# Sample states of a Mamba-2 layer: the sums over old states beside the SSD groups, the new states made in the gate and up blocks from a second read

## What is computed

```
h_new = exp(dt * A) * h_old + dt * B * x     -> output ssm_sample
y     = C . h_new + d_skip * x
```

## Time and profile before

| | |
|---|---|
| median of 3 runs | 2010.57 us (2007.6 to 2012.75) |
| profiled execution, its own time | 2014.25 us |
| its span in the profile | 2012.5 us |
| busy PE, DVE, ACT, POOL | 1912.3, 1208.4, 870.3, 202.3 us |
| mean granted TensorE clock | 0.982 |
| HBM read, written | 388.01 MB, 18.63 MB |

### The profile page before, as it was taken

How to read it: one execution, slowest core, us unless ns; L and a number is a source line. 1 busy time by engine, 2 the same in 40 slices (tenths; PEclk the granted TensorE clock), 3 DMA queues, 4 the chain that set the end, 5 groups by cost and what they waited for, 6 DMA issues and landing times.

```text
span 2012.5 us, 36117 instructions
## 1 busy us (share of the span) xinstructions
PE 1912.3 (95%) x15147; PEld 1801.3 (90%) x15147; DVE 1208.4 (60%) x1620; ACT 870.3 (43%) x1449; POOL 202.3 (10%) x124
## 2 busy tenths in 40 slices
PE   7999999997989999799899999999999999999997
PEld 5999998996888787668699989999999999999997
DVE  4367788799996655563266345655655655533434
ACT  5444455544454443452244445444444444433332
POOL 1144343443000000000000000000000000000000
PEclk9999999998999999899899999999999999999999
DMA  6578876876779697957465535555555555655452
GB/s 205 158 247 298 284 243 214 279 241 215 204 215 289 205 296 210 306 171 235 141 187 171 190 126 184 181 182 189 176 181 189 177 180 189 205 163 180 154 170 96
DMA packets 377331, 408.73 MB, mean 203 GB/s; under 512 B 10480, under 2 KB 346736, under 8 KB 376080
## 3 DMA queue, kind: packets, MB, share of 16 engines
q1 hardware_dynamic: 376608, 405.63, 63.7%
q0 software_dynamic: 208, 0.67, 0.2%
q10 hardware_dynamic: 352, 0.12, 0.0%
HBM read 388.01 MB, written 18.63 MB: 202 GB/s over the span
## 4 chain that ended last, share of the span: by engine, by line
PE 74%; DVE 10%; DMA 6%; SPq 4%; issue 3%; ACT 2%; ACTq 0%; POOL 0%; DVEq 0%; POOLq 0%
PE gemm L1548 23%; PE gemm L1549 22%; PE gemm L1550 22%; DVE w_lo L1091 3%; DMA bc<-bc_row 3%; PE side L1515 2%; DVE st L1085 1%; PE side L1787 1%; DVE conv_out L1085 1%; ACT w_hi L713 1%; SPq L494 1%; SPq L460 1%; DMA out_conv_sample<-crow 1%; DMA out_ssm_sample<-st 1%; PE side L1516 1%
## 5 line engine op out<-in xcount | busy, mean ns | idle before, releaser
L1091 DVE TENSOR_TENSOR w_lo<-raw,w_hi 128x1024 fp32r<-128x1024 f32 (+1 forms) x562 | 733.6, 1313 | 634.4 <-ACT w_hi L713 634.1
L1548 PE MATMUL gemm<-x_hi,w_hi 128*128 128x264 f32 x3344 | 978.1, 292 | 72.5 <-DVE w_lo L1091 71.1
L1549 PE MATMUL gemm<-x_lo,w_hi 128*128 128x264 f32 x3344 | 960.6, 287 | 0.0
L1550 PE MATMUL gemm<-x_hi,w_lo 128*128 128x264 f32 x3344 | 959.1, 287 | 0.0
L713 ACT ACTIVATE w_hi<-raw 128x1024 fp32r<-128x1024 f32 (+1 forms) x562 | 579.5, 1042 | 440.0 <-PE gemm L1550 438.6
L1548 PEld LDWEIGHTS gemm<-x_hi,w_hi 128*128 128x128 f32 x3344 | 641.5, 192 | 99.8 <-DVE w_lo L1091 67.4
L1549 PEld LDWEIGHTS gemm<-x_lo,w_hi 128*128 128x128 f32 x3344 | 642.5, 192 | 0.7 <-issue 0.5
L1550 PEld LDWEIGHTS gemm<-x_hi,w_lo 128*128 128x128 f32 x3344 | 639.5, 191 | 0.0
L1549 PE MATMUL gemm<-g_lo,w_hi 128*128 128x264 f32 x704 | 200.6, 285 | 0.0
L1548 PE MATMUL gemm<-g_hi,w_hi 128*128 128x264 f32 x704 | 200.2, 284 | 0.0
L1550 PE MATMUL gemm<-g_hi,w_lo 128*128 128x264 f32 x704 | 200.0, 284 | 0.0
(11 more groups left out here) (285 smaller groups left out, 1488.9 us busy)
## 6 DMA issues: line engine op xcount, KB each, us to landing
raw<-in_w_in SPq DMA_DIRECT2D x104, 1024.0 KB, 6.1
raw<-in_w_gate SPq DMA_DIRECT2D x44, 1024.0 KB, 5.1
raw<-in_w_up SPq DMA_DIRECT2D x44, 1024.0 KB, 5.1
raw<-in_w_down SPq DMA_DIRECT2D x40, 1024.0 KB, 5.4
kv<-in_cache_k SPq DMA_DIRECT2D x64, 512.0 KB, 5.9
kv<-in_cache_v SPq DMA_DIRECT2D x128, 256.0 KB, 4.3
raw<-in_w_ssm_out SPq DMA_DIRECT2D x16, 1024.0 KB, 7.4
raw<-in_w_out SPq DMA_DIRECT2D x16, 1024.0 KB, 5.4
```

Of the source, the lines that this page charges most:

```text
L1091: v.tensor_tensor(w_lo[:, s, 0:blk.kts, cols], raw[:, s, 0:blk.kts, cols], w_hi[:, b % RING, 0:blk.kts].bitcast(fp32), ALU.subtract).then_ ...
L1548: mm(out, w_hi[:, b % RING, k], pr.hi[:, x], start=(x == 0), stop=False)
L1549: mm(out, w_hi[:, b % RING, k], pr.lo[:, x], start=False, stop=False)
L1550: ins = mm(out, w_lo[:, s, k, cols], pr.hi[:, x], start=False, stop=(x == pr.kt - 1))
```

## The change

- `states` keeps only the sum over the old state: SP loads the state and the two C rows (`crows`, 128 KB) at `max(STATE[m]-6, SSD[2r]+10)`; ACT does nothing; DVE at `STATE[m]+1` waits for the load, makes `stx = st * C` and the sum. No store.
- What is missing in the sum is added per quarter: DVE multiplies the samples' B and C (`bcp`, after the convolution of c), PE sums over the partitions with `ones` at `SSD[2j]`, ACT copies to `bcd` at `+3`, and `sample_u` has three more short steps and the decay `a`.
- `new_states` makes and stores the states in the gate and up blocks, `FS[m] = B_FF + 12 + 5*m`: SP loads the state again into `st2[m % 2]` with the two B rows (`brows`, 128 KB) at `FS-4`; ACT at `FS` scales it by a in place; DVE at `FS+1` adds `B * (dt x)`, four steps; SP stores at `FS+4`.

```diff
-        bc = at("bc", [P, 2, 4, P], fp32, T0 + 8 * K)
+        crows = at("crows", [P, 4, 2, P], fp32, T0 + 8 * K)
...
+        FS = [B_FF + 12 + 5 * m for m in range(4 * NB)]
...
-                    if b == STATE[m] + 3:
-                        sp.wait_ge(st_sum, m + 1)
-                        sp.dma_start(state_rows(ho, n, r), st[:, m % 3]).then_inc(st_out[m % 3], 16)
-                    if b == STATE[m] - 3:
+                    if b == max(STATE[m] - 6, SSD[2 * r] + 10):
...
-                        wait(sp, st_out[m % 3], 16 * (m // 3))
+                        wait(sp, st_sum, m - 2)
                         sp.dma_start(st[:, m % 3], state_rows(hs, n, r)).then_inc(st_in[m % 3], 16)
-                        rows = bc_row[r].rearrange("(w b) n -> b w n", b=NB)[n]
-                        wait(sp, st_sum, m - 1)
-                        sp.dma_start(bc[:, m % 2], rows.partition_broadcast(P)).then_inc(st_in[m % 3], 16)
+                        rows = bc_row[r].rearrange("(w b) n -> b w n", b=NB)[n, 2:4]
+                        sp.dma_start(crows[:, m % 3], rows.partition_broadcast(P)).then_inc(st_in[m % 3], 16)
+
+            def new_states(b):
+
+                for m in range(4 * NB):
+                    r, n = m // NB, m % NB
+                    if b == FS[m] + 4:
+                        sp.wait_ge(s2_sum, m + 1)
+                        sp.dma_start(state_rows(ho, n, r), st2[:, m % 2]).then_inc(s2_out[m % 2], 16)
+                    if b == FS[m] - 4:
...
+                        wait(sp, s2_out[m % 2], 16 * (m // 2))
+                        sp.dma_start(st2[:, m % 2], state_rows(hs, n, r)).then_inc(s2_in[m % 2], 16)
+                        rows = bc_row[r].rearrange("(w b) n -> b w n", b=NB)[n, 0:2]
+                        sp.dma_start(brows[:, m % 2], rows.partition_broadcast(P)).then_inc(s2_in[m % 2], 16)
...
+                        if g % 2 == 0:
+                            func(bcd[:, g // 2], side[2][:, 384:400].rearrange("p (t b) -> p t b", b=NB)).then_inc(bd_cp, 1)
...
-            def states(b):
+            def new_states(b):
...
-                    if b == STATE[m]:
-                        r, n = m // NB, m % NB
-                        act.wait_ge(sx_mul, r + 1)
-                        act.wait_ge(st_in[m % 3], 32 * (m // 3 + 1))
-                        wait(act, st_sum, m)
+                    if b == FS[m]:
+                        r, n, s = m // NB, m % NB, m % 2
+                        act.wait_ge(s2_in[s], 32 * (m // 2 + 1))
                         for t in range(4):
-                            ins = func(stx[:, t, :], bc[:, m % 2, t // 2, :], scale=xdts[:, 4 * r + t, n:n + 1])
-                        ins.then_inc(stx_done, 1)
+                            ins = func(st2[:, s, t, :], st2[:, s, t, :], scale=scal[:, 4 * r + t, NB + n:NB + n + 1])
+                        ins.then_inc(s2_dec, 1)
...
-                        dve.wait_ge(stx_done, m + 1)
-                        for t in range(4):
-                            ins = stt(st[:, s, t, :], st[:, s, t, :], scal[:, 4 * r + t, NB + n:NB + n + 1], stx[:, t, :],
-                                      ALU.mult, ALU.add)
-                        drained(ins)
...
+                        dve.wait_ge(st_in[s], 32 * (m // 3 + 1))
+                        wait(dve, st_sum, m)
...
+                    if b == FS[m] + 1:
+                        r, n, s = m // NB, m % NB, m % 2
+                        dve.wait_ge(s2_dec, m + 1)
+                        for t in range(4):
+                            ins = stt(st2[:, s, t, :], brows[:, s, t // 2, :], xdts[:, 4 * r + t, n:n + 1], st2[:, s, t, :],
+                                      ALU.mult, ALU.add)
+                        ins.then_inc(s2_sum, 1)
```

More of the change, by code:

```diff
@@ L203, in bass_hybrid_decoder_layer @@
         r2b = at("r2b", [P, T], fp32, E0 + 6 * TB)
+        st2 = at("st2", [P, 2, 4, P], fp32, J1 + 2944)
+        brows = at("brows", [P, 2, 2, P], fp32, E0 + 9 * K)
         rdiag = at("rdiag", [P, 3, P], fp32, E0 + 7 * TB)
@@ L332, in bass_hybrid_decoder_layer @@
         st_in = [sem(f"st_in{s}") for s in range(3)]
-        st_out = [sem(f"st_out{s}") for s in range(3)]
+        s2_in = [sem(f"s2_in{s}") for s in range(2)]
+        s2_out = [sem(f"s2_out{s}") for s in range(2)]
         MASKS = 16
@@ L583, in side_work @@
                 states(b)
+                new_states(b)
                 key_loads(b)
@@ L605, in _ @@
                     sp.dma_start(o["y_sample"][:, 0, cols], y1s[:, cols]).then_inc(y_out, 16)
-            for s in range(3):
-                sp.wait_ge(st_out[s], 16 * len(range(s, 4 * NB, 3)))
+            for s in range(2):
+                sp.wait_ge(s2_out[s], 16 * 2 * NB)
             sp.wait_ge(k_out, 48)
@@ L1054, in side_work @@
                 ssd(b)
-                states(b)
+                new_states(b)
                 softmax(b)
@@ L1221, in conv_finish @@
                             .then_inc(xbc_done, 1)
+                    if pr.kind == "c":
+                        j = pr.idx
+                        conv_ready(dve, conv_tile("c", j, 1))
+                        wait(dve, bd_cp, j)
+                        mul(bcp[:, :, :], bct[:, j % 2, 0:2, TP:T], bct[:, j % 2, 2:4, TP:T]).then_inc(bp_done, 1)
                     if pr.kind == "x" and pr.idx % 2:
@@ L1322, in states, with new_states @@
                         r, n, s = m // NB, m % NB, m % 3
-                        dve.wait_ge(stx_done, m + 1)
-                        for t in range(4):
-                            ins = stt(st[:, s, t, :], st[:, s, t, :], scal[:, 4 * r + t, NB + n:NB + n + 1], stx[:, t, :],
-                                      ALU.mult, ALU.add)
-                        drained(ins)
-                        cb = bc[:, m % 2, 2:4, :].unsqueeze(2).to_broadcast([P, 2, 2, P])
+                        dve.wait_ge(st_in[s], 32 * (m // 3 + 1))
+                        wait(dve, st_sum, m)
+                        c = crows[:, s].unsqueeze(2).to_broadcast([P, 2, 2, P])
                         drained(mul(stx[:, :, :].rearrange("p (g t) n -> p g t n", g=2),
-                                    st[:, s].rearrange("p (g t) n -> p g t n", g=2), cb))
+                                    st[:, s].rearrange("p (g t) n -> p g t n", g=2), c))
                         v.tensor_reduce(out=ysam[:, 4 * r:4 * r + 4, n], in_=stx[:, :, :], axis=AX.X, op=ALU.add)\
                             .then_inc(st_sum, 1)
+            def new_states(b):
+                for m in range(4 * NB):
+                    if b == FS[m] + 1:
[5 more added lines that the diff above has]
+                        ins.then_inc(s2_sum, 1)
             def sample_u(b):
@@ L1341, in sample_u @@
                         xn = u[:, ts, TP:T]
+                        dve.wait_ge(bd_cp, r + 1)
+                        ys = ysam[:, ts, :]
+                        both = stx[:, 0, 0:4 * NB].rearrange("p (t b) -> p t b", b=NB)
+                        by_pair = "p (g t) b -> p g t b"
                         drained(mul(xn, xn, dskip[:, ts].unsqueeze(2).to_broadcast([P, 4, NB])))
-                        drained(v.tensor_tensor(xn, xn, ysam[:, ts, :], ALU.add))
+                        drained(mul(ys, ys, scal[:, ts, NB:2 * NB]))
+                        drained(mul(both.rearrange(by_pair, g=2), xdts[:, ts, :].rearrange(by_pair, g=2),
+                                    bcd[:, r].unsqueeze(2).to_broadcast([P, 2, 2, NB])))
+                        drained(v.tensor_tensor(ys, ys, both, ALU.add))
+                        drained(v.tensor_tensor(xn, xn, ys, ALU.add))
                         drained(mul(xn, xn, zs[:, ts, :]))
@@ L1709, in ssd @@
                             turn(side[2][:, t * P:(t + 1) * P], u[:, 2 * g + t, cols])
+                        if c == 0 and g % 2 == 0:
+                            pe.wait_ge(bp_done, j + 1)
+                            mm(side[2][:, 384:384 + 2 * NB], ones[:, :], bcp[:, :, :].rearrange("p t b -> p (t b)"),
+                               start=True, stop=True)
                         turn(side[2][:, 256:384], bc_tile(0, g)[:, cols]).then_inc(tr_mm, 1)
```

9 lines of the change are left out of this document (7 added, 2 removed).

## The result

The changed kernel takes 1960.38 us (median, 1958.81 to 1962.68) against 2011.66: a ratio of 0.9749 with an interval of 0.973 to 0.9768. The direction was right. The size was not, and of the reason given for the early gain only a part was.

A forecast was written before the change was run, and what follows sets the result against it. PE was taken as the bound, its gain lying in waits beside the SSD groups and the clock. Terms -38.5 - 8 + 1 + 17 = -28.5 took 2014.25 to 1985.7 us, median 1982; range 1964 to 2003.

The forecast's parts named there:

- What bounds the kernel: PE, busy 1912.3 of 2012.5 us; beside the SSD groups it waits 50.5 us for `w_lo`, behind ACT's waits for loads.
- Removed from the early stretch, -38.5: Beside the SSD groups, PE's 50.5 us of waits for `w_lo` were to fall to 12, a gain of 38.5 us.
- the clock, -8: Beside the SSD groups, less work at the low PE clock: 8 us of about 10 lost were to come back.
- Rival B: DVE and the SSD chain bound the early stretch: 25 of 50.5 us of waits stay, -11.5 us, 1999; chance 0.15.
- Small additions, +1: Extra short DVE, ACT and PE steps beside the SSD groups cost 1 us, bounds nothing to 5.
- rival E: GpSimd's last key products catch DVE's multiply at four pairs, at most 4 x 2.4 us on DVE: -24, 1987; chance 0.06.
- Added to the gate and up blocks, +17: The state work moved into the gate and up blocks loses 17 us: 14 from late pairs, 3 from low clock.
- the parity of m: In the gate and up blocks, even m has 3.4 us spare, odd m, whose SP turn comes one block later, 0.5.
- the eight pairs at an evacuation: m = 1, 5, 9, ... in the gate and up blocks: four late by 2.1 us, four by 1.4, 14 us together.
- L: Time from the start of SP's turn until a late pair's loads are there, in the gate and up blocks: 7.5 us.
- Rival A: Work hidden in both places, L 6 us or less and evacuations overlapping: late stage costs 4, -41.5 us, 1969; chance 0.17.
- The ring rule: In the gate and up blocks, pairs cannot land much before the weights ahead, so the late loss stays above some 6 us.

The follow-up runs named there:

- e2_short_lead: The changed kernel with the loads for the sums issued at STATE-3 in place of STATE-6: 1962.87 us, ratio 0.9787.
- e3_no_new_states: The changed kernel without new_states, so no second read, scaling or store in the gate and up blocks: 1955.51 us, ratio 0.9739.
- e6_late_lead3: The changed kernel with the late loads issued at FS-3 in place of FS-4: 1991.56 us, ratio 0.9922.
- e11_act_waits_lead6: The changed kernel, loads at STATE-6, with ACT also waiting at STATE for the landing and doing nothing with it: 1959.46 us, ratio 0.9759.
- e5_late_lead6: The changed kernel with three buffers for the late states and rows, and late loads at FS-6 in place of FS-4: 1953.79 us, ratio 0.9742.
- e1_no_stores: The kernel before the change without the 32 stores of new sample states, loads still at STATE-3: 1994.13 us beside 2007.48, ratio 0.9932.

## Why the prediction was wrong

*What bounds the kernel:* right. PE's wait beside the SSD groups went from 50.5 to 9.0 us, and the clock from 0.95 to 0.99.

*Removed from the early stretch, -38.5 and the clock, -8:* measured -51.1 (stage), where 46.5 was taken. Of it, 50.5 - 9.0 = 41.5 is waits; I put the other 10 down to the clock, as PE's busy time fell by 12 us. I had kept 12 us of waits and got 9; of the low clock 25 of 35 us went. The term was 4.6 us too small. Rival B, 25 us of waits left over, did not come.

But the reason that I gave for it was only part of the truth. I laid the gain on the wait for landings and its cure, the load three blocks earlier. The runs split it otherwise: from before, the stores take 17 us of the stage and an earlier load 20 more. What is left to the changed kernel is 14 us (18 by its second profile), and holds ACT's copies with their one buffer, DVE's steps, the row broadcast of half the size and one more block of lead; no run parts these. From the other end, putting back the bare wait costs 8 us of the stage and DVE's steps 10. These do not add up to 51. My reading, which no run tests by itself, is that each alone is absorbed by the four blocks of ring, and only what goes beyond reaches PE. In the changed kernel, with ACT out of the chain, the load could have been left at STATE-3 at little or no cost (e2_short_lead). How the stores' 17 us come about, by SP's queue or by crowding of the rings, stays open: without them both SP's issues and the landings got shorter. An earlier load with the stores in place, and a second `stx` buffer, were not run.

*Small additions, +1:* too small to be told apart from the rest of the stage. The multiply was caught by GpSimd, as rival E said, and its place was right. DVE and POOL, changed kernel:

```profile
475.73 2.06 DVE L1101 TENSOR_TENSOR stx<-st,crows 128x512 f32<-128x512 f32 x1
```

```profile
474.88 2.36 POOL L702 TENSOR_TENSOR kv<-kv,qb 128x1024 f32<-128x1024 f32 x1 [3.89 <-DMA kv<-in_cache_k]
```

The multiply ends 0.55 us after the product does, 1.4 us late. The trace has four multiplies that met a GpSimd instruction already running, two key products and two `xw` of the scan; all four end 0.55 us after it, and they are 3.1 us late in all. Four others started 0.2 us before an `xw` and kept their 0.68. This agrees with the rule of the Trainium skill, "SBUF — State Buffer", SBUF: two separate sides, that the one that starts first keeps the other waiting for its whole instruction. The price was far under the 9.6 us that I allowed, as only two met a key product, and neither from its start.

*Added to the gate and up blocks, +17:* **this is the step that failed.** It measured 4.5 us (trace) and 4.9 (e3_no_new_states beside the changed kernel's 1960.38). PE was busy 467 of 470 us there, 99%, not near 97%. The mechanism, the turns of SP, the parity of m and the eight pairs at an evacuation, was right: the five of these pairs that made PE wait and the 31 us of e6_late_lead3 follow from it. What failed is its size: the sum took all eight pairs as late by 1.4 to 2.1 us each.

Two parts of it were off. L was 6.1 to 6.5 us at five of the eight, not 7.5 (and the parts that I gave for it, 0.7 + 2 x 0.5 + 6.2, make 7.9): the broadcast of half the size landed in 5.3 us, where I had taken 6.2 from a piece with a value load on the rings, and the wait for a store held SP for 7.9 us in 18 pairs, 0.4 each and not 0.7. And the chain behind an evacuation is 0.8 to 0.9 us shorter than the sum of its parts, since ACT's and DVE's steps of the two halves overlap: m = 5 had its `w_lo` ready 14.0 us after the turn where L + 3.6 and my additions make 14.9.

The pairs were to be late by 2.1 us at an up evacuation and by 1.4 at a gate one; less 1.0 and less 0.9, that is 0.2 and nothing, and about 1.3 for m = 1, whose L was 7.6. The trace has 1.40, 0.33, 0.15 and none at the up ones, none at the gate ones with L of 6.2 to 6.5, and 0.60 and 0.49 at the two with 7.6 and 7.5. A spare near nothing, eight times over, is a threshold, and I had summed it like a price.

*How far that carries.* The profiled execution took 1962.68 us where the sum said 1985.7, 23 less. Of these 12.5 are the late term, 5.6 the early stretch with its small additions, and 5 lie in pieces outside of both, as their times vary from one execution to the next (the first and third lines of the table, mainly). With the late term right and the rest as forecast the median would have been 1969.6, inside the range; that it fell below took the other two as well, and the last of them was luck.

Rival A had the late cost right (4) and the early gain as forecast; it had 0.17. Of its two conditions the overlap of the evacuations held, and an L of 6 or less did not. The range stopped at its number with 5 us of room, and left out that the early stretch could be better at the same time.

*The ring rule.* By the Trainium skill, "DMA: Bandwidth & Descriptors", Queues, rings and completion order, each DMA engine takes the descriptors of one ring in order; from that I had it that the pair could not land much before the weights ahead of it. The gate and up weights landed in 5.3 to 5.5 us, the state issued some 0.7 us behind them in 5.2: the trace agrees, the state lands about half a microsecond after the weights. But my inference from it, that the term would not go below some 6 us, was wrong, as the term is a matter of spare and not of the landing alone.

## What to carry to other kernels

In this kernel, whose ring lets the first engine run four blocks ahead, an added wait cost nothing where it stayed under the spare of its place (e11_act_waits_lead6, e5_late_lead6) and much where it went beyond (e6_late_lead3). Where you have such a ring, work out the spare in time (due minus ready) for each parity and neighbour, and where a spare is near zero, put both outcomes for all its pairs into the range. Ask which engine stands in a wait, and not only how long: the same late landings cost 8 us of the stage more when ACT stood in them (67 us) than when only DVE did (29 us). Where a load comes late, try one more buffer with an earlier issue (3.5 to 4.5 us of the stage here).

## What the runs showed that I had not expected

The 32 stores of 256 KB, for which SP waited 3.9 us in all and no other engine waited, were worth 13 us of the whole (e1_no_stores). And one block of lead, 2.9 us, decided between 4.5 us of loss and 36 (e6_late_lead3), since SP does its side work in turns of two blocks.
